# A linear-recurrence block on one core: sixteen projection tiles in high and low halves, channels in two halves, four branch tiles in the gates' banks

## The reference

```
gate_br, rec = split(h @ w_in)            # 1024 -> 2 x 1024, h is the normalised input
gate_br = gelu(gate_br)
xc = causal_depthwise_conv(rec, conv_w, conv_b)          # 4 taps
r = sigmoid(block_diag_linear(xc, w_r, b_r))             # 4 blocks of 256 x 256
i = sigmoid(block_diag_linear(xc, w_i, b_i))
log_a = -8 * r * softplus(-lam);  a = exp(log_a)
u = sqrt(-expm1(2 * log_a)) * i * xc
hs[t] = a[t] * hs[t-1] + u[t]
return (hs * gate_br) @ w_out
```

## Time and profile before

| | us |
|---|---|
| median of 3 runs (1596.39 to 1597.03) | 1596.45 |
| the profiled execution | 1597.79 |
| its span in the trace | 1596.0 |
| PE / PEld busy | 1557.8 / 1347.4 |
| DVE / ACT / POOL busy | 1048.9 / 736.5 / 926.0 |

### The profile page before, as it was taken

One profiled execution on the slowest core, in us unless ns is written; L12 is line 12 of the kernel. 1 busy time (PEld: TensorE's weight loads), 2 busy tenths in 40 slices (PEclk: granted clock), 3 DMA queues, 4 the chain that ended last, 5 costly groups with the idle time before them and its releaser, 6 DMA issues.

```text
span 1596.0 us, 24610 instructions
## 1 busy us (share of the span) xinstructions
PE 1557.8 (98%) x9578; PEld 1347.4 (84%) x9578; DVE 1048.9 (66%) x1432; ACT 736.5 (46%) x1071; POOL 926.0 (58%) x1090
## 2 busy tenths in 40 slices
PE   9999999999999999999999999999999999899998
PEld 7888888877788888888888788888888888778887
DVE  6866555755886669976355886657676655378663
ACT  6554442023554555555252554555555544355542
POOL 6966520202886677975102886667976661178764
PEclk9999999999999999999999999999999999999999
DMA  7655533222565554665344565564555561246553
GB/s 273 209 188 184 186 110 103 80 79 81 176 208 194 163 197 157 195 204 190 131 154 145 179 206 194 163 209 152 173 198 190 169 202 40 72 163 215 190 166 119
DMA packets 107203, 263.65 MB, mean 165 GB/s; under 512 B 9168, under 2 KB 43088, under 8 KB 106960
## 3 DMA queue, kind: packets, MB, share of 16 engines
q1 hardware_dynamic: 107088, 262.09, 49.6%
HBM read 261.00 MB, written 1.05 MB: 164 GB/s over the span
## 4 chain that ended last, share of the span: by engine, by line
PE 88%; DVE 6%; ACT 3%; POOL 2%; issue 1%; DMA 0%; SPq 0%; DVEq 0%; ACTq 0%
PE ps L1613 39%; PE ps L1614 22%; PE ps L1661 9%; PE ps L1707 5%; PE ps L1616 4%; POOL w_lo L521 2%; DVE arena L1563 1%; PE ps L2114 1%; PE ps L1904 1%; PE ps L1645 1%; PE ps L1806 1%; PE ps L1646 1%; PE ps L1647 1%; DVE xn L916 1%; ACT w_hi L599 1%
## 5 line engine op out<-in xcount | busy, mean ns | idle before, releaser
L521 POOL TENSOR_TENSOR w_lo<-raw,w_hi 128x256 fp32r<-128x256 f32 x1056 | 907.3, 893 | 554.4 <-ACT w_hi L599 551.1
L1613 PE MATMUL ps<-xn,w_hi 128*128 128x512 f32 x1848 | 661.0, 396 | 10.8 <-DVE arena L995 3.6
L1614 PE MATMUL ps<-xn,w_lo 128*128 128x256 f32 x2112 | 552.0, 281 | 0.0
L599 ACT ACTIVATE w_hi<-raw 128x1024 fp32r<-128x1024 f32 (+1 forms) x492 | 450.7, 926 | 192.8 <-PE ps L1616 106.8
L1613 PEld LDWEIGHTS ps<-xn,w_hi 128*128 128x128 f32 x1848 | 346.4, 187 | 91.5 <-DVE xn L916 5.4
L1614 PEld LDWEIGHTS ps<-xn,w_lo 128*128 128x128 f32 x2112 | 398.4, 189 | 16.8
L1613 PE MATMUL ps<-hid,w_hi 128*128 128x512 f32 x1008 | 363.6, 397 | 1.3 <-DVE w_lo L908 1.3
L1614 PE MATMUL ps<-hid,w_lo 128*128 128x256 f32 x1056 | 292.5, 282 | 0.0
L908 DVE TENSOR_TENSOR w_lo<-raw,w_hi 128x512 fp32r<-128x512 f32 (+1 forms) x222 | 255.7, 1152 | 33.7 <-ACT w_hi L599 28.8
L1613 PEld LDWEIGHTS ps<-hid,w_hi 128*128 128x128 f32 x1008 | 190.1, 189 | 42.7 <-issue 1.6
L995 DVE TENSOR_TENSOR arena<-ps,low_part 128x512 f32<-128x512 f32 x132 | 90.7, 687 | 183.8 <-ACT low_part L667 183.7
(11 more groups left out here) (320 smaller groups left out, 1225.4 us busy)
## 6 DMA issues: line engine op xcount, KB each, us to landing
raw<-blocks SPq DMA_DIRECT2D x419, 512.0 KB, 3.6
raw<-blocks SPq DMA_DIRECT2D x144, 256.0 KB, 3.5
cst<-consts SPq DMA_DIRECT2D x1, 2358.0 KB, 15.5
x<-x_in SPq DMA_DIRECT2D x4, 256.0 KB, 7.3
out<-x SPq DMA_DIRECT2D x4, 256.0 KB, 3.3
cst<-consts SPq DMA_DIRECT2D x1, 109.0 KB, 2.0
```

Of the source, the lines that this page charges most:

```text
L521: ins = nc.gpsimd.tensor_tensor(w_lo[:, slot(n), piece], raw[:, slot(n), piece], w_hi[:, slot(n), piece], ALU.subtract)
L599: nc.scalar.activation(w_hi[:, slot(n), cols], raw[:, slot(n), cols], ACT.Copy)\
L1613: nc.tensor.matmul(where, hi, both.rearrange("p a t -> p (a t)"), start=opens, stop=False)
L1614: ins = nc.tensor.matmul(where[:, 0:SEQ], lo, high, start=False, stop=False)
```

## The change

The sixteen blocks of lru_in and lru_branch become split blocks (kind `split_in`), so PE does three products of `head_tiles` in the place of each raw product, ACT makes sixteen more `hi` and POOL sixteen more `lo`. The norm ahead of the block makes `xn` halves (ACT `high_halves`, DVE `low_halves`) in the place of `xs`. The first two tiles run together, not four, and the sum of squares stands after the seventh input tile. Gates and branch share one list, `lru_mid`: gate blocks 0 and 1, branch 0 to 3, gate blocks 2 and 3, branch 4 to 7. Branch tiles 4 to 7 go into banks 4 to 7 and wait for the gates' sigmoids on their bank (`lru_ri`). The output rows stay raw and read the product from `lru_gate` in the place of `y`. ACT and DVE work by halves of four channel tiles, two squares move from DVE to ACT (L812 and L817 of the new kernel), and ACT's `hi` stand between the gates' functions.

```
+LRU_ORDER = (0, 1, 4, 5, 6, 7, 2, 3, 8, 9, 10, 11)
-    add("lru_in", ["in"] * 8)
-    add("lru_gates", ["lru"] * 4)
-    add("lru_branch", ["in"] * 8)
+    add("lru_in", ["split_in"] * 8)
+    add("lru_mid", ["split_in" if at >= 4 else "lru" for at in LRU_ORDER])
...
-DIRECT_GAINS = ("g_mix", "g_lru")
+DIRECT_GAINS = ("g_mix",)
... (POOL)
+                if phase.startswith("lru"):
+                    for n in range(n0, LAST[phase]):
+                        if is_split(n):
+                            lo(n)
... (ACT)
+                hi_until(n0 + 7)
+                preload(ACT.Sigmoid)
+                hi_until(lru_branch_block(2))
+                gates(0)
+                gates(1)
+                hi_until(lru_branch_block(3))
+                gates(2)
+                gates(3)
+                need(act, "lru_sp", 1)
+                tanhs(0)
+                decays(0)
+                hi_until(lru_branch_block(4))
+                root(0)
+                gate_squares(0)
+                hi_until(lru_branch_block(5))
+                preload(ACT.Sigmoid)
+                hi_until(lru_branch_block(6))
+                gates(4)
+                gates(5)
+                hi_until(lru_branch_block(7))
+                gates(6)
+                gates(7)
+                gelu(0)
+                tanhs(1)
+                decays(1)
+                root(1)
+                gate_squares(1)
+                gelu(1)
... (DVE)
+                for i in range(KD):
+                    convolved(i)
+                    if i == 1:
+                        softplus()
+                gated(0)
+                branch(0)
+                branch(1)
+                decayed(0)
+                branch(2)
+                branch(3)
+                cubic(0)
+                gated(1)
                 scan_inputs(0)
+                branch(4)
+                scan(0)
+                branch(5)
+                scan(1)
+                decayed(1)
                 branch(6)
+                scan(2)
+                branch(7)
                 cubic(1)
                 scan(3)
                 scan_inputs(1)
... (PE)
+                together = 2 if norm == "g_lru" else 4
...
-                projections(FIRST["lru_in"], "g_lru", KD, LRU_SPARE)(KD - 4)
+                projections(FIRST["lru_in"], "g_lru", KD, LRU_SPARE)(KD - 2)
+                def branch(i):
+                    need(pe, *(("proj_out", before + 4 + i + 1) if i < 4 else ("lru_ri", i + 1)))
+                    head_tiles([(lru_branch_block(i), ps[:, branch_bank(i), 0:SEQ])], xn)
+                gates(0)
+                gates(1)
+                for i in range(4):
+                    branch(i)
+                gates(2)
+                gates(3)
+                for i in range(4, KD):
+                    branch(i)
...
-                need(pe, "proj_out", before + 2 * KD)
+                need(pe, "proj_out", before + KD + 4)
                 for i in range(KD):
                     need(pe, "y_ready", i + 1)
-                    add_direct(n, y[:, i, :], start=i == 0, stop=i == KD - 1)
+                    add_direct(FIRST["lru_out"] + i, lru_gate[:, i, :], start=i == 0, stop=i == KD - 1)
```

More of the change, by code:

```diff
@@ L777, in gates, with tanhs @@
                         .then_inc(ev["lru_ri"], 1)
[L779 to L786, removed]
+                def tanhs(half):
+                    act.wait_ge(ev["lru_ri"], 4 * half + 4)
                     for i in range(4 * half, 4 * half + 4):
@@ L790, in lru, with decays, gate_squares, root @@
                     chain(ins)
+                def decays(half):
                     for i in range(4 * half, 4 * half + 4):
                         ins = nc.scalar.activation(lru_a[:, i, :], lru_a[:, i, :], ACT.Exp, scale=sp[:, 2, i:i + 1])
-                    ins.then_inc(ev["lru_a"], 1)
-                for half in range(2):
+                    chain(ins)
+                    fours = slice(4 * half, 4 * half + 4)
+                    nc.scalar.activation(rec[:, fours, 0:SEQ], lru_a[:, fours, :], ACT.Square).then_inc(ev["lru_a"], 1)
+                def gate_squares(half):
+                    need(act, "proj_out", TAKEN_BEFORE["lru_in"] + KD + 4 * half + 4)
+                    fours = slice(4 * half, 4 * half + 4)
+                    nc.scalar.activation(gelu_z[:, fours, :], lru_gate[:, fours, :], ACT.Square).then_inc(ev["lru_sq"], 1)
+                def root(half):
                     fours = slice(4 * half, 4 * half + 4)
@@ L888, in _ @@
                 lambda: (norm(3, "both", after="ffn_b", behind=FIRST["ffn_c"] + 5), ffn(2, FIRST["ffn_c"])),
-                lambda: (norm(5, "g_lru", ACT.Sigmoid, after="ffn_c"), lru()),
+                lambda: (norm(5, "g_lru", ACT.Exp, after="ffn_c", behind=FIRST["lru_in"] + 5), lru()),
                 lambda: (norm(6, "g_ffn_d", late=(0, FIRST["ffn_d"] + 3, FIRST["ffn_d"] + 4)), ffn(3, FIRST["ffn_d"])),
@@ L1426, in lru, with softplus, gated @@
                             signal(ins, "lru_xc")
-                n0 = FIRST["lru_branch"]
-                halves = [slice(0, 4), slice(4, 8)]
-                def branch(first):
-                    for i in (first, first + 1):
-                        take(n0 + i, i % 4, lru_gate[:, i, :])
+                def softplus():
+                    need(v, "lru_ln", 1)
+                    chain(tsc(sp[:, 0, :], const("lam"), -1.0, 0.0, ALU.mult, ALU.max))
+                    chain(tt(sp[:, 0, :], sp[:, 0, :], sp[:, 1, :], ALU.add))
+                    chain(tsc(sp[:, 2, :], sp[:, 0, :], -LRU_C, None, ALU.mult))
+                    signal(tsc(sp[:, 3, :], sp[:, 0, :], LRU_C, None, ALU.mult), "lru_sp")
+                halves = [slice(0, 4), slice(4, 8)]
+                def branch(i):
+                    take(lru_branch_block(i), branch_bank(i), lru_gate[:, i, :])
+                def gated(half):
+                    need(v, "lru_ri", 4 * half + 4)
+                    chain(tt(lru_h[:, halves[half], :], lru_i[:, halves[half], :], xc[:, halves[half], :], ALU.mult))
                 def decayed(half):
```

63 lines of the change are left out of this document (27 added, 36 removed).

## The result

The changed kernel takes **1584.89 us** in the median of four runs (1584.74 to 1587.11), where the kernel before took 1596.42 beside it (1596.27 to 1597.03). The ratio is 0.9928, with a 95% interval of 0.9916 to 0.9940. A second set on another chip gave 1585.07 (1583.95 to 1585.84) against 1596.93, 0.9926 [0.9912, 0.9939]. The forecast was 1585.8, so it was 0.9 too slow. The profiled execution took 1585.02.

A forecast was written before the change was run, and what follows sets the result against it. PE's own instruction list (busy 1557.8 of 1596.0 us) and one hole were taken as the bound. -9.19 - 1.71 + 0.26 = -10.6 us off the median 1596.45 gave 1585.8, own range 1584.6 to 1587.3, chance 0.62.

The forecast's parts named there:

- The products: lru_in and branch on PE: 128 raw products at 0.432 us become three instructions each, 0.360 us: 9.19 us less.
- Rival D: Split products on PE do not pay, three instructions taking 0.432 us: 1594.7; chance 0.07, shared with anything near no change.
- The hole: PE's gap before the output rows, 0.44 us DVE take plus 1.27 issue, goes if `y_ready` 1 is in time: 1.71 us.
- The start: PE's wait for the sum of squares at the stage's start: bounds 0 and 0.53 us, 0.26 taken.
- DVE beside POOL: DVE's eight convolutions slowed by POOL's pieces: 7.7 us more, the eighth ending at 814.7, no wait of PE at gates.
- Rival A: Each POOL piece costs DVE 0.55 us, decay argument late, PE waits 3.8 us at branch tile 4: 1589.6; chance 0.22.
- The slack behind the convolutions: DVE's time in hand before branch tile 4: 0.8 us at ACT's square, 0.9 at gate half 4, 1.7 in all.
- rival B: POOL bounds: at 4.8 us a block, later low halves are 1 to 3 us late for PE: 1588; chance 0.05.
- Rival C: Slower than before: DVE and POOL block each other all stage, a convolution tile over 4.9 us: about 1599; chance 0.04.
- The tail: DVE's scans before the output rows: `y_ready` 1 at 835.5, wanted 838.2; `y_ready` 4 at 844.7, wanted 848.6; no wait.

The follow-up runs named there:

- e1_raw: The changed kernel with the sixteen blocks back to raw products, new order and banks kept: 1595.08 us, 0.9987 against 1596.43 for the kernel before.
- e5_dve_plus5: The changed kernel with the gated input of half 0 computed six times on DVE, not once: 1591.95 us, ratio 0.9969 to the kernel before.
- e7_four: The changed kernel with four first tiles together and the sum of squares after the third input tile again: 1590.09 us, ratio 0.9954 to the kernel before.
- e4_dve_plus2: The changed kernel with the gated input of half 0 computed three times on DVE, not once: 1587.54 us, ratio 0.9939 to the kernel before.
- e6_six_pieces: The changed kernel with two extra POOL pieces ahead of each of the sixteen blocks, six for four: 1601.80 us against 1596.95 for the kernel before.

## Why the prediction was right, point by point

- **The products**: -9.19 worked out; 9.1 by e1_raw in the trace. The spacing of 0.120 us is that of the earlier trace rows. Rival D (1594.7) is out: e1_raw, which is that case, took 1595.08.
- **The hole**: -1.71 was the term. The whole stage, less the products, gained 1.9 to 2.0. By the spacing of the products, PE's last one ends at 847.32, and the rows start at 849.25: 1.93. The chain counts 0.44 + 1.27 and leaves the last 0.2 with PE. The term was 0.2 too small. Its reading was wrong too: the 1.27 us are not issue but DVE's scan and product of tile 0, for which row 0 waited (848.00 to 849.15). The banks alone could not have taken that away. By the trace it is the halves, which let these two steps run ahead of the last takes: `y_ready` 1 came at 834.4, 2.3 us before the rows. No run undid the halves alone. The prediction had this as a condition ("if `y_ready` 1 is there in time"), and its check of the tail is what carried the term.
- **The start**: +0.26 was the term, the wait was 0. DVE was done with the sum's input at 780.89 and PE came to it at 780.97, 0.08 us to spare. The times were as close as the prediction said, and the middle of the bounds was a value that neither case has. This and the hole are some 0.5 of the 0.9 us by which the forecast was too slow. The rest is of the size of what moves in stretches that the change does not touch.
- **DVE beside POOL**: 7.7 us worked out, 7.9 measured up to the end of the convolutions; first take and eighth convolution within 0.1 us of the schedule once that is moved by PE's earlier start (775.94 for 777.5). Three steps cost 1.07 more (1.0 had been taken), the tiny steps 1.9 in all (up to 1.3 had been). That the sum is so close is in part luck: the softplus steps cost 1.9 and not 1.3, the rest 6.0 and not 6.4. Rival A's 0.55 us for each piece did not come.
- **The slack behind the convolutions**: 0.8 + 0.9 = 1.7 us worked out, 1.27 + 1.0 = 2.3 read, and 2.3 by two doses.
- **Rival A** had the right chain, but not the whole price: with 13.2 us instead of 7.7 PE would have waited some 3.2 us, and may have paid for it by the clock again. e5_dve_plus5 shows that at a wait of 5.6, e7_four at 1.9; e4_dve_plus2, at 1.8, does not.
- **POOL (rival B)** is where the working was weak. The forecast needed the low halves in time, and they were, but not with "about 3 us or more everywhere". Up to branch block 3 a piece took 0.79 to 0.87; block 4 had 0.96 and blocks 5 to 7 had 1.02, beside DVE's steps of 1024 columns, where 0.84 had been taken for all. Branch block 7, with 3.3 us in hand by the schedule (832 against 835.3), had 0.5. That the time came out was close to luck here: 0.5 us more and PE waits, as in e4_dve_plus2. Also, the price of 1588 at 4.8 us a block was wrong: e6_six_pieces at 5 us took 1601.8. The step that failed was to take POOL's lateness as 1 to 3 us once; it grows with every block, and brings a lower clock. So the chance of 0.05 and the price both understated this rival. The range would not have held that case. Rival C, slower than before, was put down to DVE alone; the run that was slower came from POOL.
- **The tail**: `y_ready` 1 at 834.4 and 4 at 843.7, wanted at 836.8 and 847.1; the schedule, moved, had 833.9 and 843.1. No wait, as said.

What stays open: why the clock dips in the attention stage and behind the k/v projection differ from one kernel to the next, and why a wait of 1.9 us was followed by the lower clock in e7_four and one of 1.8 us in e4_dve_plus2 was not. They were seen, not tried. No experiment moved POOL's last margin of 0.5 us by itself.

## What to carry to other kernels

When PE is busy throughout, first count what it is given to do: three 0.120 us instructions for one product of 0.432 were 9 of the 11 us, and the engines that paid for it (POOL 64 pieces, DVE 7.9 us of contention) had the time. Lay the other engines against PE's new schedule and know the smallest slack of each; here it is 2.3 us for DVE at the decay argument, 2.1 at gate block 1, and only 0.5 for POOL at the last branch block. Do it to the end of the stage, with the lengths that the steps have beside each other there, and not with a mean from elsewhere. Count that a new wait of PE can cost more than its length, and a slow supplier every unit it supplies.

## What the runs showed of the hardware that I had not expected

- A wait of PE can cost more than itself. After 5.6 us of waiting, PE worked for some 3 us at a granted clock of 0.50 (1.2 GHz), and 1.8 us were lost on top; after 1.9 us in e7_four it was 0.50 too, also 1.8 lost; after 1.8 us in e4_dve_plus2 the windows show 1.00, and only about 0.2 was lost at the restart. So waits of nearly the same length differ in this.
- A DVE step on 8 columns takes 0.17 us alone and 0.59 to 0.66 beside POOL: nearly a POOL piece's length for almost no work, and of about the same added time as a one-input step of 256 columns (0.41 to 0.96). Only steps that read PSUM kept their 0.42.
- Added DVE steps of 1024 columns took 1.22 us each alone; three of them in a row beside POOL took 4.58, and POOL's four pieces in the same stretch of e5_dve_plus5 6.56, where they are 3.82 in after and 2.78 with DVE quiet. The contention is paid on both sides, and the longer the DVE step, the more a piece beside it takes: 0.9 us beside steps of 256 columns, 1.7 beside steps of 1024.
